# U projection with the weights stationary, u turned to its state layout through DRAM

## The reference, cut to what matters

```python
h = rms_norm(x, lw['norm_mix_g'])
proj = h @ lw['w_in']
q, k, v, u, g_att, g_s5 = jnp.split(proj, IN_SPLITS, axis=-1)
s5y, hT_re, hT_im = s5_scan(u, h0_re, h0_im, ...)

ug = u.reshape(Bsz, L, S5_GROUPS, S5_CH)
bu_re = jnp.einsum('blgc,gpc->blgp', ug, bb_re)
bu_im = jnp.einsum('blgc,gpc->blgp', ug, bb_im)
_, _, hr, hi = lax.associative_scan(combine, (ar, ai, bu_re, bu_im), axis=1)
```

## Time and profile before

| what | value |
|---|---|
| median of 3 runs | 4048.93 us (4039.6 to 4050.96) |
| the profiled execution's own time | 4048.68 us |
| its span, first to last instruction | 4046.9 us |
| mean granted TensorE clock | 0.919 of 2.4 GHz |
| PE busy | 3448.2 us (85%) |
| DVE busy | 2982.2 us (74%) |
| ACT busy | 1573.7 us (39%) |
| POOL busy | 1083.1 us (27%) |

### The profile page before, as it was taken

The page is one execution under the profiler, slowest core; times in us unless marked ns, Lnnn a source line. Parts: engine busy times, 40 slices in busy tenths (PEclk is TensorE's granted clock), DMA queues, the critical chain, the costliest instruction groups (busy, mean ns, idle before and its releaser), DMA issues. The chain is left out here.

```text
span 4046.9 us, 48282 instructions
## 1 busy us (share of the span) xinstructions
PE 3448.2 (85%) x15934; PEld 2298.5 (57%) x15934; DVE 2982.2 (74%) x5688; ACT 1573.7 (39%) x3899; POOL 1083.1 (27%) x879
## 2 busy tenths in 40 slices
PE   8989998897778779887677758796869999999998
PEld 5757876544444445355466644353436666666665
DVE  6584113788978778889766778799858787787765
ACT  2233421435663234376533323325853323333232
POOL 0100001332233333422232323332333333333331
PEclk9989998998889889998888879897989999999999
DMA  3023457998879999977799999897999999999996
GB/s 143 8 79 127 140 179 263 366 418 322 321 276 419 362 397 401 415 272 279 280 361 361 362 344 374 321 377 267 357 393 405 416 415 416 415 417 415 411 416 255
DMA packets 296235, 1311.76 MB, mean 324 GB/s; under 512 B 39442, under 2 KB 99314, under 8 KB 189618
## 3 DMA queue, kind: packets, MB, share of 16 engines
q0 software_dynamic: 120272, 854.67, 53.3%
q1 hardware_dynamic: 175330, 453.87, 29.7%
q10 hardware_dynamic: 384, 0.13, 0.0%
HBM read 1249.94 MB, written 56.79 MB: 323 GB/s over the span
## 5 line engine op out<-in xcount | busy, mean ns | idle before, releaser
L1036 POOL DMA_INDIRECT arena<-in_uv,arena x800 | 1027.7, 1285 | 2272.5 <-DVE arena L1202 2038.8
L726 PE MATMUL ps<-arena 128*128 128x256 f32 (+2 forms) x3456 | 1104.3, 479 | 163.7 <-DMA arena<-in_w_stat 90.1
L1192 DVE CUSTOM_DVE_ANT_0 arena<-arena 128x1024 f32<-128x1024 f32 x800 | 973.7, 1219 | 49.8 <-DMA arena<-in_uv,arena 46.0
L1202 DVE SCALAR_TENSOR_TENSOR arena<-arena 128x1024 f32<-128x1024 f32 x736 | 943.1, 1281 | 80.3 <-ACT arena L1293 79.0
L726 PEld LDWEIGHTS ps<-arena 128*128 128x128 f32 x3456 | 674.8, 199 | 548.9 <-issue 330.6
L1284 ACT ACTIVATE arena<-arena 128x2 f32<-128x2 f32 x400 | 80.8, 202 | 1156.3 <-DVE arena L1192 1139.6
L2673 PE MATMUL ps<-arena 128*128 128x256 f32 x2048 | 470.1, 383 | 0.0
L2682 PE MATMUL ps<-arena 128*128 128x512 f32 x1024 | 460.0, 592 | 0.0
L2673 PEld LDWEIGHTS ps<-arena 128*128 128x128 f32 x2048 | 384.5, 193 | 48.7 <-issue 0.5
L2682 PEld LDWEIGHTS ps<-arena 128*128 128x128 f32 x1024 | 194.6, 190 | 191.1 <-issue 184.6
L2798 DVE TENSOR_TENSOR arena<-arena 128x256 f32<-128x256 f32 x128 | 79.7, 623 | 269.7 <-ACT arena L2763 233.6
(11 more groups left out here) (297 smaller groups left out, 4041.5 us busy)
## 6 DMA issues: line engine op xcount, KB each, us to landing
arena<-in_uv SPq DMA_DIRECT2D x256, 512.0 KB
arena<-in_w_stat SPq DMA_DIRECT2D x216, 512.0 KB
arena<-in_cache_k SPq DMA_DIRECT2D x64, 512.0 KB
arena<-in_cache_v SPq DMA_DIRECT2D x64, 512.0 KB
arena<-in_w_mov SPq DMA_DIRECT2D x14, 2048.0 KB, 13.1
scr_w<-arena SPq DMA_DIRECT2D x8, 2048.0 KB
arena<-scr_w SPq DMA_DIRECT2D x16, 1024.0 KB
arena<-in_uv,arena POOLq DMA_INDIRECT x800
```

The costliest lines, as they stand in the source:

```text
L726: last = nc.tensor.matmul(ps[:, bank, 0:w], wbuf[m % NWB][:, kc * P:(kc + 1) * P], moving[:, kc, :], start=(kc == 0), stop=(kc == KC - 1))
L1036: pool.indirect_dma_start(ring[s % RING], None, dr["uv"], bass.IndirectOffsetOnAxis(ap=idx[:, g % 4, j:j + 1], axis=0)).then_inc(row_in[s ...
L1192: nc.vector.tensor_tensor_reduce(ring[s % RING][:, 0:D], ring[s % RING][:, 0:D], h2r[:, b % 2, :], 1.0, 0.0, ALU.mult, ALU.add, act_in[:, ...
L1202: nc.vector.scalar_tensor_tensor(accr[:, b % 2, :], ring[s % RING][:, D:2 * D], wgt[:, s % RING:s % RING + 1], accr[:, b % 2, :], ALU.mult ...
```

## The change

The weights become the stationary operand and all 1,056 tokens move, in three groups of 352. For each of 8 tiles `j` of 128 output channels PE runs 3 groups of 8 matmuls into 3 banks. ACT copies each bank to a staging buffer `u_st` (two of them) with the 8 places of a chunk apart, and the 32 sample tokens of the last group to `us_st`. SP writes tile `j` to two DRAM scratch tensors, and reads it back in the layout of `ug`, straight to its partitions, in four parts: tiles 0 to 3 after tile 4 is written, 4 and 5 after tile 6, tile 6 after tile 7, tile 7 last. The transposes, the small matmuls and their ACT copies are gone. The third block's rounds wait for the part that they read. `hT` moves to the place of `m_toe`, so that `ug` can be filled while the projection runs; the zeroing of `m_toe` now waits for the projection's end and the spill, and the zeroing of the small part of `ug` moves to the start of POOL's list.

```diff
-        hT = lay(AT_UG, [KC, T])
+        hT = lay(AT_TOE, [KC, T])
...
-        u_tok = lay(AT_TOE, [G, ST8, CH])
-        us_tok = lay(AT_HH, [G, NNEW, CH])
-        us_st = lay(AT_HH, [D])
+        u_st, us_st = lay(AT_HH, [2, ST8, P]), lay(AT_HH + 2 * D, [KC, NNEW, NSEQ])
...
+        U_PARTS = ((0, 4), (4, 6), (6, 7), (7, KC))
+        scr_u = nc.dram_tensor("scr_u", (D, ST8, P), F32, kind="Internal").ap()
+        scr_us = nc.dram_tensor("scr_us", (D, NNEW, NSEQ), F32, kind="Internal").ap()
+        W_U = T // 3
+        N_U = W_U // ST8
...
-                sp.wait_ge(u_free, ST8 + 2)
-                sp.dma_start(scr_us, us_st[0:NS, :]).then_inc(us_out, 16)
-                sp.wait_ge(us_out, 16)
-                for t in range(NNEW):
-                    sp.dma_start(us_tok[0:NSEQ, :, t, :], scr_us.rearrange("(q t) (g c) -> t q g c", t=NNEW, c=CH)[t]).then_inc(us_in, 16)
+                def tiles_in(part):
+                    lo, hi = U_PARTS[part]
+                    for m in range(2):
+                        sp.wait_ge(u_out[m], 32 * ((hi + 1 - m) // 2))
+                    gs = slice(lo * P // CH, hi * P // CH)
+                    for t in range(ST8):
+                        sp.dma_start(ug[CH * t:CH * (t + 1), gs, 0:P], scr_u.rearrange("(g c) t n -> t c g n", c=CH)[t, :, gs]
+                                     ).then_inc(ug_in[part], 16)
+                    for t in range(NNEW):
+                        sp.dma_start(ug[64 + CH * t:64 + CH * (t + 1), gs, P:NUG],
+                                     scr_us.rearrange("(g c) t q -> t c g q", c=CH)[t, :, gs]).then_inc(ug_in[part], 16)
+
+                for j in range(KC):
+                    sp.wait_ge(u_free, 3 * j + 3)
+                    sp.dma_start(scr_u[j * P:(j + 1) * P], u_st[:, j % 2]).then_inc(u_out[j % 2], 16)
+                    sp.dma_start(scr_us[j * P:(j + 1) * P], us_st[:, j]).then_inc(u_out[j % 2], 16)
+                    for part in range(len(U_PARTS)):
+                        if U_PARTS[part][1] == j:
+                            tiles_in(part)
+                tiles_in(len(U_PARTS) - 1)
                 sp.wait_ge(spill, 16)
+                sp.wait_ge(ug_zero, 1)
                 sp.wait_ge(k_d, 2)
...
-                pool.wait_ge(u_ready, NU)
-                nc.gpsimd.memset(ug[0:64, :, P:NUG], 0.0).then_inc(toe_zero, 1)
-                pool.wait_ge(ug_ready, G // 4)
+                pool.wait_ge(u_ready, 3 * KC)
...
+                for j in range(KC):
+                    pe.wait_ge(slab_in[j // 4], 16)
+                    if j >= 2:
+                        pe.wait_ge(u_free, 3 * (j - 1))
+                    for third in range(3):
                         for kc in range(KC):
+                            last = nc.tensor.matmul(ps[:, 3 * (j % 2) + third, 0:W_U], slab[:, j // 4, kc, (j % 4) * P:(j % 4 + 1) * P],
+                                                    hT[:, kc, W_U * third:W_U * (third + 1)], start=(kc == 0), stop=(kc == KC - 1))
                         last.then_inc(u_ready, 1)
+                pe.wait_ge(u_free, 3 * KC)
...
+                for j in range(KC):
+                    if j >= 2:
+                        act.wait_ge(u_out[j % 2], 32 * (j // 2))
+                    for third in range(3):
+                        n0, bank = N_U * third, 3 * (j % 2) + third
+                        n = min(N_U, P - n0)
+                        act.wait_ge(u_ready, 3 * j + third + 1)
+                        last = nc.scalar.activation(u_st[:, j % 2, :, n0:n0 + n].rearrange("p t n -> p n t"),
+                                                    ps[:, bank, 0:n * ST8].rearrange("p (n t) -> p n t", t=ST8), ACT.Copy)
+                        if n < N_U:
+                            last = nc.scalar.activation(us_st[:, j].rearrange("p t q -> p q t"),
+                                                        ps[:, bank, n * ST8:W_U].rearrange("p (q t) -> p q t", t=NNEW), ACT.Copy)
+                        last.then_inc(u_free, 1)
...
-                dve.wait_ge(ug_ready, G // 4)
+                dve.wait_ge(spill, 16)
+                dve.wait_ge(u_ready, 3 * KC)
...
                 for gp in range(GP):
                     if gp + 1 < GP:
                         transposes(gp + 1)
+                    for part, (lo, hi) in enumerate(U_PARTS):
+                        if 2 * gp == lo * P // CH:
+                            pe.wait_ge(ug_in[part], 16 * (ST8 + NNEW))
```

More of the change, by code:

```diff
@@ L95, in hybrid_step @@
         NUG = P + NSEQ
-        AT_CL, AT_TOE, AT_WS, AT_HS, AT_HH, AT_H0, AT_KS, AT_PW, AT_UG = np.cumsum(
-            [0, GP * 2 * 9 * CH, G * P, G * P + 512, 2 * GP * NSEQ, 2 * GP * (NCH + 1), 2 * GP * NSEQ,
+        AT_CL, AT_TOE, AT_HS, AT_WS, AT_HH, AT_H0, AT_KS, AT_PW, AT_UG = np.cumsum(
+            [0, GP * 2 * 9 * CH, G * P, 2 * GP * NSEQ, G * P + 512, 2 * GP * (NCH + 1), 2 * GP * NSEQ,
              G * P, 9 * 2 * GP]).tolist()
-        hT = lay(AT_UG, [KC, T])
+        hT = lay(AT_TOE, [KC, T])
         xt = lay(0, [TT + 1, D])
@@ L271, in hybrid_step @@
         u_ready, u_free = sem("u_ready"), sem("u_free")
-        ug_ready, ug_free = sem("ug_ready"), sem("ug_free")
+        U_PARTS = ((0, 4), (4, 6), (6, 7), (7, KC))
+        u_out, ug_in = [sem(f"u_out{k}") for k in range(2)], [sem(f"ug_in{k}") for k in range(len(U_PARTS))]
         par_a, par_v, spill = sem("par_a"), sem("par_v"), sem("spill")
-        scr_us = nc.dram_tensor("scr_us", (NS, D), F32, kind="Internal").ap()
-        us_out, us_in = sem("us_out"), sem("us_in")
+        scr_u = nc.dram_tensor("scr_u", (D, ST8, P), F32, kind="Internal").ap()
+        scr_us = nc.dram_tensor("scr_us", (D, NNEW, NSEQ), F32, kind="Internal").ap()
         k_ready, k_free, k_d, cl_ready = sem("k_ready"), sem("k_free"), sem("k_d"), sem("cl_ready")
-        toe_zero, toe_in, low_zero = sem("toe_zero"), sem("toe_in"), sem("low_zero")
-        NU = 2 * ST8 + 2
-        U_STEPS = (ST8, *range(ST8))
+        toe_zero, toe_in, low_zero, ug_zero = sem("toe_zero"), sem("toe_in"), sem("low_zero"), sem("ug_zero")
+        W_U = T // 3
+        N_U = W_U // ST8
         def complex_step(dve, mul, re, im, ar, ai, br, bi, sign, t):
@@ L313, in _ @@
             def _(pool):
+                nc.gpsimd.memset(ug[0:64, :, P:NUG], 0.0).then_inc(ug_zero, 1)
                 pool.wait_ge(spill, 16)
-                pool.wait_ge(u_ready, NU)
-                nc.gpsimd.memset(ug[0:64, :, P:NUG], 0.0).then_inc(toe_zero, 1)
-                pool.wait_ge(ug_ready, G // 4)
-                pool.wait_ge(toe_zero, 1)
+                pool.wait_ge(u_ready, 3 * KC)
+                pool.wait_ge(ug_zero, 1)
                 nc.gpsimd.memset(m_toe[32:64], 0.0)
@@ L323, in _ @@
             def _(pe):
[L324 to L330, removed]
+                for j in range(KC):
[3 more added lines that the diff above has]
+                    for third in range(3):
                         for kc in range(KC):
-                            tok = hT[:, kc, s:SEQ:ST8] if s < ST8 else hT[:, kc, SEQ:T]
-                            last = nc.tensor.matmul(ps[0:rows, n % 4, :], tok, slab[:, k, kc, :],
-                                                    start=(kc == 0), stop=(kc == KC - 1))
+                            last = nc.tensor.matmul(ps[:, 3 * (j % 2) + third, 0:W_U], slab[:, j // 4, kc, (j % 4) * P:(j % 4 + 1) * P],
+                                                    hT[:, kc, W_U * third:W_U * (third + 1)], start=(kc == 0), stop=(kc == KC - 1))
                         last.then_inc(u_ready, 1)
[L336 to L345, removed]
+                pe.wait_ge(u_free, 3 * KC)
                 pe.wait_ge(cl_ready, 1)
@@ L358, in _ @@
                     last.then_inc(k_ready, 1)
[L359 to L363, removed]
             @block.scalar
@@ L395, in _ @@
                                              ACT.Copy).then_inc(k_free, 1)
-                act.wait_ge(ug_ready, G // 4 + 1)
-                nc.scalar.activation(ug[64:P, :, P:NUG], ps[64:P, 7, :].rearrange("p (g q) -> p g q", g=G), ACT.Copy).then_inc(ug_free, 1)
             @block.vector
@@ L1381, in hybrid_step @@
         spent = [ident_in, const_in, lam_in, *x_in, ss_zero, sq_done, ms_done, rt_done, rc_done, sq_dve, f_done, take_dve, take_act, xT_done,
-                 lam_v, lam_a, par_in, *slab_in, us_out, us_in, u_ready, u_free, ug_ready, ug_free, par_a, par_v, spill, k_ready, k_free,
+                 lam_v, lam_a, par_in, *slab_in, u_ready, u_free, *u_out, *ug_in, ug_zero, par_a, par_v, spill, k_ready, k_free,
                  k_d, cl_ready, toe_zero, toe_in, wT_ready, wT_free, se_ready, se_free, sp_out, ss_out, rec, hh_zero, y_ready, y_free,
```

## The result

The changed kernel took 4013.03 us in the median of 6 runs (4006.92 to 4020.24), the kernel before 4041.51 us in the median of 6 on the same chip (4031.27 to 4050.96): a ratio of 0.9942, 95% interval 0.9923 to 0.9962. The medians lie 28.5 us apart, which is the sum that was forecast; that they agree to the tenth is luck, since the interval of the ratio spans 15 to 31 us. The profiled execution took 4006.92 us. One further execution of the changed kernel, among those of experiment 9, took 5149.58 us at a mean granted clock of 0.643 and is left out of every comparison.

What follows compares the result with a forecast made beforehand. The prediction took PE to bound the second block, until DVE, POOL or SP becomes its last. Gains of 10.8 + 7.6 + 10.1 = 28.5 us from 4048.7 gave 4020 us, with an 8-in-10 range of 4009 to 4035.

Steps and rivals of the forecast that it cites:

- Projection: Second block: 384 passes of 352 columns replace 288 of 512, taking 116.3 us; gain 10.8 us, from 9.9 to 10.9.
- Turning: Between projection and chunk kernels: 8.5 us go, a 0.9 us wait for ACT's last copies comes; gain 7.6 us.
- Chunk kernels: Second block, after the projection: 14.25 us as before, no gain.
- DVE has no slack left: Second block: DVE's own work ends at 149.8 us, level with the projection's end.
- a projection still shorter would gain nothing: Second block: shortening the projection further gains 0, because DVE's own work ends level with it.
- Sample tokens: Second block's end: without the 64 small matmuls and their copy, the third block follows DVE's last addition; gain 10.1 us.
- Through DRAM: SP's writes and reads beside the second block: 26 issues of 0.48 us after the projection, hidden; cost 0.
- the rival that SP becomes last: Second block's end: SP's issuing holds the block; decides from 0.62 us an issue, about 4107 us; 5%.
- The rate of 92 GB/s: Reads from DRAM: 4.2 MB take 46 us, landing before their rounds; cover lost below half that rate.
- Third block's clock: Third block's start: half clock as before, 0 us; rival, no drop, gains about 3 us, 4017 us, 10%.
- All that follows is shifted as a whole: From the third block on: everything starts earlier by what the second block saves, 28.5 us.
- The rival that the shift is given back in full: Blocks after the second: later waits absorb up to all of 28 us, giving 4035 to 4049; 10%.

Runs made afterwards that it cites:

- experiment 9: Both kernels unchanged, for second profiles and more times: profile spans 4031.6 us (kernel before) and 4016.5 us (changed kernel); ratio 0.9932.
- Experiments 3 and 4: 3: changed kernel with the projection's last eighth left out, 4021.43 us. 4: the same, with POOL's fills waiting for DVE's first zeroing, 4031.12 us. One time each.
- experiment 1: Kernel before without the sample tokens' 64 small matmuls and ACT's copy of them, POOL zeroing their place: 4041.1 us, one time.
- Experiment 2: Changed kernel with one part instead of four, all reads issued after the last tile is written: 4043.58 us, ratio to the kernel before 1.0011.
- Experiment 7: Changed kernel with three idle matmuls of 512 columns behind the chunk kernels: 4010.86 us, ratio to the kernel before 0.9919.

## Why the prediction was right, point by point

*Projection, 10.8 us.* The term measured 11.77 us in the first profile, above its range of 9.9 to 10.9, and, with a projection of 116.73 us against 127.17, 10.4 in the second. Over the six executions with this projection it lasted 115.2 to 116.9 us, where 116.3 was predicted. The pass of 352 columns takes what the line said: two of ACT's copies, 16 passes apart, lie 149.59 - 144.85 = 4.74 us from each other, 0.296 a pass. What differs between the two profiles is the start: the clock rose earlier in the first (0.67 as the mean granted clock from 33.6 to 38.7 us, where the earlier trace rows and the second profile had 0.50). Seen from behind, the gain is one of columns: 288 x 512 = 147,456 went to 384 x 352 = 135,168, because the 32 sample tokens no longer take a full pass to themselves; the 12,288 between them are 10.3 us at 0.429 for 512.

*Turning, 7.6 us.* Measured 7.64. The copies took 0.72 and 0.26 us for the 0.7 and 0.2 assumed; the step in ACT's writes was rightly priced from DVE's.

*Chunk kernels, unchanged.* 14.15 us for 14.25, and 16.57 for 16.7 to the end of the addition. "DVE has no slack left" was right (it became free at 150.10, 0.55 us behind the projection, and 0.57 ahead of it in the second profile), but "a projection still shorter would gain nothing" missed half: POOL's fills hang on the projection's end and, if they meet DVE's last single-input instructions, hold them. Experiments 3 and 4 show that cost, 10.2 us; in the changed kernel itself it is nothing.

*Sample tokens, 10.1 us.* 9.92, in the changed kernel and by itself in experiment 1. The change of block took 0.50 us, not the 0.27 that was read from ACT's last copy.

*Through DRAM, nothing.* Right in the sum, but with less to spare than its working said. The 26 issues after the projection took 163.77 + 1.85 - 150.38 = 15.24 us, 0.59 each, where 0.48 was assumed. The reads among them took 0.46 to 0.68 us each with 128 packets, against 0.48 with 512 in the earlier trace rows, so fewer packets did not make an issue cheaper. The prediction put the rival that SP becomes last at 0.62, but 16.7 / 26 is 0.64. So 1.4 us, not "some 4", kept that rival out. Its mechanism, an issue that waits for room, is there in the first part of the reads:

```profile
108.70 8.73 SPq L309 DMA_DIRECT2D arena<-scr_u  x8
...
117.47 9.07 SPq L312 DMA_DIRECT2D arena<-scr_us  x4
121.71 0.26 ACT L381 ACTIVATE arena<-ps 128x32 f32<-128x32 f32 x1
126.59 1.43 SPq L317 DMA_DIRECT2D scr_u<-arena  x1
```

These 12 issues of 512 packets took up to 2.3 us each, and held the write of the next tile from 121.97 to 126.59; the second staging buffer covered that. Experiment 2 is this rival made real, at 3.5 us an issue of 1,024 packets. The rate of 92 GB/s was a fair bound: with all reads together, in experiment 2, the DMA moved 99 GB/s from 154.4 to 200 us, and in the changed kernel PE waited for no read. The estimate of 109 that the prediction worked out from the Trainium skill ("SBUF — State Buffer", "Door 1: The DMA port swizzle") lies 10% above that measurement.

*Third block's clock, 0.* Right: three rounds took 1.18 us and then 0.68, as in the earlier trace rows. In the second profile the clock fell a little later (two slow rounds instead of three) and the recurrence came 1 us sooner; in neither did it stay up. Experiment 7 has the price of that rival, 1.4 to 2.4 us for the 3 assumed.

*All that follows is shifted as a whole.* Right in the mean, not in any single pair of profiles: the means lie 27.6 us apart in the first set of runs and 26.5 in the second (experiment 9). The rival that the shift is given back in full is out; that some microseconds of it are isn't excluded, as the intervals go down to 15 us.

## What to carry to other kernels

When a layout change goes through DRAM, count the issues that must come after the last producer and price them on a queue that is already full, because the block can't end before the queue's engine has issued the last of them. Before shortening the stage that sets a block's end, look at what is released by that end: here POOL's fills, which would have caught DVE in its last small instructions. And judge a gain of 0.7% at the stage where it arises, in the timeline, since two executions of the kernel before differed by 17 us in the stages behind it.

## What the runs showed of the hardware beside that

PE's clock returned at different times in executions of the same program. The fourth block's matmuls start at 267.9 us in both profiles of the changed kernel, after PE had stood 11.2 us; two stretches of the first profile, and the later one in the second (columns of the earlier trace rows):

```profile
272.90:277.90 5.00, 5.00 (x36) 4.05 (x35) 4.96 (x6) 0.99 (x10) 0.00 (x0) 0.67 0.00 0
277.90:282.90 5.00, 5.00 (x50) 4.19 (x46) 4.93 (x6) 1.91 (x18) 0.00 (x0) 1.00 0.00 2
```

```profile
277.90:282.90 5.00, 5.00 (x27) 3.91 (x25) 4.93 (x6) 1.44 (x13) 0.00 (x0) 0.50 0.00 2
```

Half speed lasted some 8 us in the one and about 21 in the other, and the stage, from the first to the last of its 128 passes on `ug`, took 49.2 and 54.9 us. Over all profiles of this study it took 47.6 to 55.1 us, whatever the kernel: 7 us of spread from one such stage.
